# Two transformer blocks on one core: window scores from one key tile, gate tile 0 split on VectorE, bias and meta maps of the differential attention moved on GpSimd

## The reference

```python
def first_block(...):                       # branch a: window and sinks; branch b: top-k over latents
    aq, ak, av, bq, bkv, iq, ik, iw, gates = jnp.split(proj, IN_SPLITS, axis=-1)
    o_a = sliding_window_sink_attention(aq, ak, av, sinks[l], bias_a)
    ik = layer_norm(ik, ...)                # keys of the indexer: logits = iq . ik, relu, weighted sum, top 128
    o_b = indexed_sparse_mla(q_abs, c_kv, iq, ik, iw, w_uv[l], bias_b)
    mixed = gate_a * (o_a @ w_branch_a[l]) + gate_b * (o_b @ w_branch_b[l])

def diff_attn_rows(q1, q2, k1, k2, v, qpos, kpos, key_real, slopes, lam):      # second block, branch a
    bias = -slopes[:, None, None] * (abs(qpos[:, None] - kpos[None, :]) * key_real[None, :])[None]
    s1 = einsum('bqhd,bkhd->bhqk', q1, k1) * scale + bias
    s2 = einsum('bqhd,bkhd->bhqk', q2, k2) * scale + bias
    attn = softmax(s1) - lam * softmax(s2)
    return einsum('bhqk,bkhe->bqhe', attn, v)                     # 4 heads, 4 blocks of 128 rows, 16 + 512 keys

def window_attn_blocks(q, k, v, qpos, kpos, kvalid, kreal, slopes, sink):      # second block, branch b
    # a block of 128 rows sees the 16 meta keys, its own block, the block before and the block after
    s = einsum('bnqgrd,bnkgd->bngrqk', q, k) * scale - slopes * dist           # 8 heads, 2 key groups
    ...
```

## Time and profile before

| | us |
|---|---|
| median of 3 runs | 1560.12 |
| lowest, highest | 1557.65, 1564.45 |
| the profiled execution | 1559.88 |
| its span in the trace | 1558.1 |
| PE busy in the span | 1523.6 (98%) |
| DVE busy | 846.3 (54%) |
| ACT busy | 533.3 (34%) |
| POOL busy | 242.2 (16%) |

### The profile page before, as it was taken

One profiled execution on the slowest core, in us unless ns is written; L12 is line 12 of the kernel. 1 busy time (PEld: TensorE's weight loads), 2 busy tenths in 40 slices (PEclk: granted clock), 3 DMA queues, 4 the chain that ended last, 5 costly groups with the idle time before them and its releaser, 6 DMA issues.

```text
span 1558.1 us, 21063 instructions
## 1 busy us (share of the span) xinstructions
PE 1523.6 (98%) x7388; PEld 1239.9 (80%) x7388; DVE 846.3 (54%) x1519; ACT 533.3 (34%) x942; POOL 242.2 (16%) x190
## 2 busy tenths in 40 slices
PE   7999999999999999999999999999999999999998
PEld 6867887877788888888899778788787888888876
DVE  5577895466555355445854383544655543553454
ACT  5124445523332123222511363444333222221223
POOL 2323334340000000000003473221400000000000
PEclk9999999999999999999999999999999999999999
DMA  6524420023333333332323202111333333333322
GB/s 150 150 54 121 146 62 1 8 88 108 94 94 95 95 94 92 97 92 86 92 86 90 54 15 68 55 54 35 101 95 94 94 96 93 94 94 95 94 81 95
DMA packets 250283, 132.61 MB, mean 85 GB/s; under 512 B 21225, under 2 KB 247653, under 8 KB 250222
## 3 DMA queue, kind: packets, MB, share of 16 engines
q1 hardware_dynamic: 247998, 123.92, 28.0%
q0 software_dynamic: 2144, 7.77, 1.6%
q10 hardware_dynamic: 80, 0.14, 0.0%
HBM read 129.67 MB, written 6.38 MB: 87 GB/s over the span
## 4 chain that ended last, share of the span: by engine, by line
PE 89%; DVE 5%; issue 2%; ACT 1%; DMA 1%; POOL 1%; SPq 0%; DVEq 0%; ACTq 0%; POOLq 0%
PE psL L1715 61%; PE psL L1854 11%; PE psS L1715 5%; PE psT L1863 2%; PE psL L1982 1%; PE psS L2126 1%; PE psS L1959 1%; PE psS L1889 1%; DMA xin<-in_x 1%; PE psS L1902 1%; PE psL L2084 1%; POOL wl L572 1%; PE psS L2103 1%; POOL biasD L650 0%; PE psS L1876 0%
## 5 line engine op out<-in xcount | busy, mean ns | idle before, releaser
L1715 PE MATMUL psL<-hn,wh 128*128 128x512 f32 x1680 | 530.0, 397 | 1.1 <-POOL wl L572 0.9
L1715 PEld LDWEIGHTS psL<-hn,wh 128*128 128x128 f32 x1680 | 314.7, 188 | 77.3 <-issue 1.5
L696 ACT ACTIVATE wh<-stage 128x1024 fp32r<-128x1024 f32 (+3 forms) x250 | 243.3, 973 | 336.8 <-PE psL L1715 244.0
L1715 PE MATMUL psL<-hn,wl 128*128 128x512 f32 x840 | 331.1, 394 | 0.0
L1032 DVE TENSOR_TENSOR wl<-stage,wh 128x1024 fp32r<-128x1024 f32 (+1 forms) x168 | 201.2, 1198 | 92.7 <-ACT wh L696 88.0
L1715 PE MATMUL psL<-hid,wh 128*128 128x512 f32 x704 | 221.6, 395 | 1.3 <-DVE wl L1032 1.3
L572 POOL TENSOR_TENSOR wl<-stage,wh 128x1024 fp32r<-128x1024 f32 (+2 forms) x82 | 156.8, 1912 | 327.0 <-ACT wh L696 327.0
L1715 PEld LDWEIGHTS psL<-hn,wl 128*128 128x128 f32 x840 | 158.5, 189 | 35.6
L1854 PE MATMUL psL<-hn,wh 128*128 128x512 f32 x496 | 172.9, 430 | 1.9 <-POOL wl L572 1.8
L1715 PEld LDWEIGHTS psL<-hid,wh 128*128 128x128 f32 x704 | 131.4, 187 | 35.1 <-DVE wl L1032 3.0
L1715 PE MATMUL psL<-hid,wl 128*128 128x512 f32 x352 | 138.9, 395 | 0.0
(11 more groups left out here) (384 smaller groups left out, 1977.5 us busy)
## 6 DMA issues: line engine op xcount, KB each, us to landing
stage<-in_w_in SPq DMA_DIRECT2D x54, 512.0 KB, 3.9
stage<-in_w_ffn_gate SPq DMA_DIRECT2D x22, 512.0 KB, 3.8
stage<-in_w_ffn_up SPq DMA_DIRECT2D x22, 512.0 KB, 3.8
stage<-in_w_ff_gate SPq DMA_DIRECT2D x22, 512.0 KB, 3.8
stage<-in_w_ff_up SPq DMA_DIRECT2D x22, 512.0 KB, 3.8
stage<-in_w_out SPq DMA_DIRECT2D x16, 512.0 KB, 3.8
stage<-in_w_ffn_down SPq DMA_DIRECT2D x16, 512.0 KB, 3.9
stage<-in_w_ff_down SPq DMA_DIRECT2D x16, 512.0 KB, 3.9
```

The costliest lines, as they stand in the source:

```text
L696: act.activation(wh[:, b, 0:n], stage[:, b, 0:n], ACT.Copy).then_inc(hi[b], 1)
L1715: ins = pe.matmul(dst, w[:, b, k * P:(k + 1) * P], x[:, part, k, c0:c1], start=k + n == 0, stop=k == kc - 1 and n == 2)
```

## The change

**Keys once more.** ACT copies the keys into `kbm`, which is the tile `ikz` of the first block under another name: keys 0 to 255, the 16 meta keys, keys 256 to 511. It does so with three copies between the query projections. The window scores of blocks 0 and 3 are then one matmul of 272 columns from `kbm`.

**Gate tile 0.** In block 1 DVE splits gate tile 0, between the third and fourth eviction of `uq1`, and ACT copies gate tile 1 after the relu of logit 12 instead of at the start of the window loop.

**The differential attention.** `biasD` becomes two tiles, used by even and odd blocks; POOL writes them head by head, six heads ahead of the loop and the rest between other steps, and waits only from block 2 on. The copies into `m8d` move from ACT to POOL, one in each step, and `biasW` is spread between them. On DVE the reciprocal of unit j - 1 goes between the two biased maps of unit j. PE's wait for the last query evictions moves from before the loop to step 3.

```diff
@@ tensors
+        kbm = ikz
+        biasD1, o = at("biasD1", [P, 4, NKEY], o)      # behind vm8, in the space of the gates
-        biasD, o = at("biasD", [P, 4, NKEY], o)
+        biasD0, o = at("biasD0", [P, 4, NKEY], o)
+        biasD = (biasD0, biasD1)
@@ gpsimd, gates of block 1
-                low_pair("gates1", i)
+                if i == 0:
+                    low("gates1", i, 1)
+                else:
+                    low_pair("gates1", i)
@@ gpsimd, block 2
-            def bias_block(i):
-                if i:
-                    pool.wait_ge(ph["df"]["neg"], 8 * i)
-                for h in range(4):
-                    pool.tensor_scalar(biasD[:, h, META:NKEY], dist[...], ..., None, ALU.mult).then_inc(biasD_ok, 1)
+            def bias_unit(j):
+                i, h = divmod(j, 4)
+                if i >= 2:
+                    pool.wait_ge(ph["df"]["neg"], 8 * (i - 1))
+                pool.tensor_scalar(biasD[i % 2][:, h, META:NKEY], dist[...], ..., None, ALU.mult).then_inc(biasD_ok, 1)
+
+            def stack_maps_meta(u):
+                i, h = divmod(u, 4)
+                pool.wait_ge(df_sum, u + 1)
+                if h == 0 and i >= 2:
+                    pool.wait_ge(ph["df"]["pt"], META_TURN[4][i - 2] + 1)
+                pool.tensor_copy(m8d[:, i % 2, h * META:(h + 1) * META], W6[:, u % 3, 0, 0:META]).then_inc(ph["df"]["meta"], 1)
...
-            bias_window(0, NH // 2)
-            bias_block(2)
-            bias_window(NH // 2, NH)
-            bias_block(3)
+            for u in range(2, 16):
+                stack_maps_meta(u)
+                if 4 <= u < 12:
+                    bias_unit(u + 4)
+                elif u < 4:
+                    bias_window(2 * u - 4, 2 * u - 2)
+                else:
+                    bias_window(u - 8, u - 7)
@@ scalar
             high("gates1", 0, 0)
-            relu_of(11, 16)
+            relu_of(11, 13)
+            high("gates1", 0, 1)
+            relu_of(13, 16)
...
+            def middle_meta():
+                act.wait_ge(ev[0], PAIR0["kv2"] + PAIRS["kv2"])
+                act.activation(kbm[:, :, 0:NEAR], kbz[:, :, META:META + NEAR], ACT.Copy)
+                act.activation(kbm[:, :, NEAR:NEAR + META], kbz[:, :, 0:META], ACT.Copy)
+                act.activation(kbm[:, :, NEAR + META:], kbz[:, :, META + NEAR:NKEY], ACT.Copy).then_inc(kbm_ok, 1)
...
-                    act.activation(m8d[:, i % 2, h * META:(h + 1) * META], W6[:, u % 3, 0, 0:META], ACT.Copy).then_inc(p["meta"], 1)
@@ vector
             take_scaled("uq1", 1, 0, qT[:, 2, :], sq[:], QSCALE)
+            low("gates1", 0, 0, ())
             add_logits(11, 12)
...
+                        if m and j:
+                            reciprocal_of(j - 1)
@@ tensor
-            for b in range(2):
-                pe.wait_ge(ev[b], PAIR0["gates2"])
...
+                if j == 3:
+                    for b in range(2):
+                        pe.wait_ge(ev[b], PAIR0["gates2"])
...
+                    if i == 0:
+                        keys = kbm[:, h // 4, 0:NEAR + META]
+                    elif i == NB - 1:
+                        keys = kbm[:, h // 4, NEAR:NKEY]
+                    elif wcol == META:
+                        keys = k[:, 0:META + W]
                     else:
-                        pe.matmul(psS[:, 2 * (j % 2), mcol:mcol + META], q, k[:, 0:META], start=True, stop=True)
-                        ins = pe.matmul(psS[:, 2 * (j % 2), wcol:wcol + W], q, k[:, k0:k0 + W], start=True, stop=True)
+                        keys = k[:, k0:NKEY + META]
+                    ins = pe.matmul(psS[:, 2 * (j % 2), 0:META + W], q, keys, start=True, stop=True)
```

More of the change, by code:

```diff
@@ L665, in _ @@
             pool.wait_ge(dist_ok, 2)
[L666 to L670, removed]
+            for tile in biasD:
+                pool.memset(tile[:, :, 0:META], 0.0)
+            low("qb2", 0, 0)
+            bias_unit(0)
+            low("qb2", 0, 1)
+            bias_unit(1)
+            low("qb2", 1, 0)
+            bias_unit(2)
+            low("qb2", 1, 1)
+            for j in range(3, 6):
+                bias_unit(j)
+            pool.wait_ge(zeros, 2)
+            stack_maps_meta(0)
+            bias_unit(6)
+            stack_maps_meta(1)
+            bias_unit(7)
             pool.wait_ge(nat_t, 3)
@@ L783, in _ @@
             high("gates1", 0, 0)
-            relu_of(11, 16)
+            relu_of(11, 13)
+            high("gates1", 0, 1)
+            relu_of(13, 16)
             def gate_high(l, j):
                 for step in range(2 * KD):
-                    if GATE_START[l][step] == j:
+                    if GATE_START[l][step] == j and (l == 2 or step):
                         if step % 2 == 0:
@@ L1602, in _, with reciprocal_of @@
             p = ph["df"]
+            def reciprocal_of(u):
+                v.wait_ge(ph["df"]["p"], 2 * u + 2)
+                v.reciprocal(st[:, 6, 0:1], rsum[:, 2 * u + 1:2 * u + 2]).then_inc(recip_ok, 1)
             for j in range(16 + 5):
@@ L1613, in _ @@
                         biased(p, u, as_halves(W6[:, j % 3, m, :], NKEY), two_banks(psS[:, 2 * m:2 * m + 2, :], NKEY),
[L1614 removed]
+                               as_halves(biasD[i % 2][:, h, :], NKEY), -TAKEN, u)
+                if j == 16:
+                    reciprocal_of(15)
                 if 1 <= j < 17:
                     u = j - 1
[L1617 to L1618 removed]
+                    v.wait_ge(recip_ok, u + 1)
                     dv.link(v.scalar_tensor_tensor(out=st[:, 6, 1:2], in0=rsum[:, 2 * u:2 * u + 1], scalar=st[:, 6, 0:1], in1=neglam[:],
@@ L2096, in _ @@
                     k0 = META + P * lo_c
-                    if lo_c == 0 and wcol == META:
-                        ins = pe.matmul(psS[:, 2 * (j % 2), 0:META + W], q, k[:, 0:META + W], start=True, stop=True)
-                    elif k0 + W == NKEY and mcol == W:
-                        ins = pe.matmul(psS[:, 2 * (j % 2), 0:W + META], q, k[:, k0:NKEY + META], start=True, stop=True)
-                    else:
-                        pe.matmul(psS[:, 2 * (j % 2), mcol:mcol + META], q, k[:, 0:META], start=True, stop=True)
-                        ins = pe.matmul(psS[:, 2 * (j % 2), wcol:wcol + W], q, k[:, k0:k0 + W], start=True, stop=True)
+                    if i == 0:
+                        if j == 0:
+                            pe.wait_ge(kbm_ok, 1)
+                        keys = kbm[:, h // 4, 0:NEAR + META]
[3 more added lines that the diff above has]
+                        keys = k[:, 0:META + W]
+                    else:
+                        keys = k[:, k0:NKEY + META]
+                    ins = pe.matmul(psS[:, 2 * (j % 2), 0:META + W], q, keys, start=True, stop=True)
                     ins.then_inc(p["s"], 1)
```

19 lines of the change are left out of this document (7 added, 12 removed).

## The result

The changed kernel takes 1553.11 us (median of 7 runs, 1548.66 to 1555.29), the kernel before 1562.85 in the 7 runs beside it: 0.9942, 95% interval 0.9923 to 0.9961. The same program twice more, on two chips: 0.9958 (0.9944 to 0.9972) and 0.9935 (0.9921 to 0.9949). The kernel before stood 2.7 us higher in those 7 runs than the 1560.12 from which the forecast subtracts, so the ratios are the safer comparison. The profiled execution took 1552.76 us with a span of 1551.0, against 1559.88 and 1558.1.

The account below looks back on a forecast made before the run. PE, busy for 98% of the span, was taken to bound the kernel. Gate tiles 2.6, window scores 3.1 and differential attention 2.8 sum to 8.5 us off 1560.12, giving 1551.6 us; 8-in-10 range 1548.5 to 1556.0.

Parts of the forecast that it names:

- Gate tiles 0 and 1: Block 1: PE's waits of 0.88 and 1.75 us for POOL's splits go entirely, at no cost; 2.6 us.
- Window scores: Block 2's window attention: 16 fused units cost 0.31 instead of 0.52 us, all but the first counting; 3.1 us.
- Rival 3: Window scores: the 16-column matmul already lay beside others, so 0.8 us saved instead of 3.1; 1553.9 us, chance 0.08.
- Differential attention: PE's idle pieces in block 2's differential attention shrink; 2.8 us less, between 1.6 and 3.5.
- The moved wait: Before the first differential score: PE's 0.83 us wait for the last query evictions, moved to step 3, goes; gain 0.8.
- the split out of the loop: Differential attention: PE's 1.36 us wait for DVE's difference map, held by POOL's gate tile split, goes; gain 1.4.
- the small waits: Differential attention: PE's other waits for difference maps and ACT's turned maps shrink; 0.6 us taken of a possible 1.2.
- The clock: Differential and window attention of block 2: granted clock 1.00, full speed, in both, with no change of it taken.
- Rival 1: Differential attention: DVE's factor waits about 1 us in two steps with `biasW` pairs; 2.0 given back, 1553.6 us, chance 0.15.
- Rival 2: POOL misses block 2's gate tile 0, or block 1's earlier split delays sums; 2 to 3 us back, 1554.2, chance 0.14.
- Rival 4: Differential attention: POOL becomes the bound, slower than before, some 1568 us, needing a copy of 2.2 us; chance 0.03.

Follow-up runs that it names:

- the third profile: The changed kernel run a third time, unchanged: 0.9935 (0.9921 to 0.9949), clock 1.00 throughout the differential attention, stage 50.68 us.
- the kernel without PE's 0.40: Changed kernel, but PE's wait before block 2's window loop asks for block 2's normalised output first, the last part one step later: 1551.18 us, 0.9930.

## Why the prediction was right, point by point

The forecast was 1551.6, within 1548.5 to 1556.0, with "faster" the likeliest. The median of 1553.11 lies in the range; the ratio of 0.9942 is just beyond the half per cent, with an interval that reaches to both sides of it, and the two repeats (0.9958 and 0.9935) lie on either side. That it is less than before is clear; that it is more than half a per cent less is not.

- **Gate tiles 0 and 1, 2.6 us.** Right, and low: by their own rows 2.0 us at tile 1, where the wait shown was 1.75, and 1.2 at tile 0 (1.48 to 0.32), where it was 0.88, 3.2 in all. The modelled end of the matmul ahead of each covers the rest of either gap. The times of the steps were as worked out: copy at 114.81 (estimated 115), POOL's split over at 118.32 (118.5), the sum for logit 12 held until 118.88 (118.5), at no cost.
- **Window scores, 3.1 us.** Right: 2.98, and 0.31 us a unit. The first unit's gain came back as a longer wait for `yn`, 0.40 us instead of 0.20, as forecast. Rival 3 falls.
- **Differential attention, 2.8 us.** The mechanisms were right, the size was not. Without the fall of the clock it is 0.9 ahead of the first score and 3.1 in the stage, 4.0, above the upper bound of 3.5. The moved wait gave 0.9 (0.8 predicted), the split out of the loop 1.4 to 1.5 (1.4). For the small waits that leaves 1.6 to 1.7 where 0.6 was taken and 1.2 thought possible: that term was mis-sized. Putting the reciprocal back costs 0.35 of it, putting the copies back on ACT 0.46 (51.03 and 51.14 against 50.68). Its waits in brackets fell by 1.1: the three small ones for the difference map, 0.7, are gone, and of those for ACT's turned maps 0.4 (0.59 to 0.20; the 1.5 of the earlier trace rows is the whole program's, and 0.88 of it lies in block 1). The rest never stood in a bracket: from the kernel before with PE's wait moved to the third profile the shown waits of the stage fell by 2.2 us (3.8 to 1.6), PE's idle time by 2.4 (4.03 to 1.65) and its busy time, for nearly the same number of records, by 0.8, together the 3.1. The likely reason, which no run isolates, is that the modelled end of a matmul reaches into the wait behind it and hides part of it, so that a sum over brackets lacks that part.
- **The clock.** "The granted clock is 1.00 in both, full speed, and I take no change of it" is the step that failed. In the profiles of the changed kernel, two of three, it fell to half for 7.6 us and took 2.6 of the 4.0. What the runs show in its place is a clock that comes and goes between executions of the same program. With the fall the profiled execution is 7.1 us faster than before (8.5 predicted), without it 9.4. The forecast lies between the two by no merit of its own: the small waits gave 1.0 more than predicted and the fall took 2.6.
- **The rest.** Predicted at nothing, 0.5 us come back behind the window loop of block 2 (467.12 to 467.64): it comes in at four tiles of the branch projections, 0.25 us at the first, where PE waits 0.20 for POOL's split, which it did not before. POOL waits there for ACT: ACT's step on `mix` starts 0.40 us behind the DVE instruction that releases it (1083.33 to 1083.73), 0.12 in the kernel before (1091.01 to 1091.13), and the copy of the tile stands behind it. The kernel with the meta copies on ACT doesn't have it (467.12), which cancels the 0.46 that it loses in the stage; but the kernel with the differential part alone doesn't have it either (467.13), and it copies on POOL. Why ACT starts later stays open.
- **Rival 1** (POOL blocks DVE for whole instructions, bias heads too) falls: no PE wait of 1 us appears in the steps with two `biasW` heads. The timelines of POOL and DVE in the kernel after show a factor and a difference that begin inside a bias head:

```profile
910.06 1.49 POOL L657 TENSOR_SCALAR biasD<-dist 128x512 f32<-128x512 f32 x1
```

```profile
911.08 0.21 DVE L1660 SCALAR_TENSOR_TENSOR st<-rsum,st,neglam 128x1 f32<-128x1 f32 x1
911.33 0.77 DVE L1662 SCALAR_TENSOR_TENSOR W<-W,st 128x528 f32<-128x528 f32 x1
```

Both take what they take elsewhere (0.22 and 0.77 us); the factor is over 0.26 us before the head (911.55). The longest factor in the stage of after is 0.55 us, at 927.18, beside the start of a head at 927.22, and it too ends 0.66 before that head does. The weight split, however, did hold DVE to its last 0.02 us. The Trainium skill (SBUF — State Buffer, "SBUF: two separate sides") has exclusion for the whole instruction. The 2.00 us factor beside the split, a POOL instruction with two inputs, agrees with it; the 0.21 us factor inside a bias head, which reads one input, does not.
- **Rival 2** (POOL late in the tail) did not come, but the margin was as thin as stated: predicted 0.2, measured 932.25 against 932.46. In the kernel without PE's 0.40 it was down to 0.08.
- **Rival 4:** a copy takes 0.20 us, a tenth of its point.

## What to carry to other kernels

An instruction that holds another engine costs what is waiting behind that engine: move it to where the held engine has slack. When both the medians and a trace must judge an edit of 1 us, compare stage by stage between landmarks, and read the granted clock of each stage first: one fall of the clock, 2.6 us, was about as large as a whole part of this change. And a chain of small steps can lose more to small waits than its list of waits shows: here the brackets fell by 2.2 us and the stage by 3.1.

## What the runs showed of the hardware

PE's clock fell in a stretch in which PE itself was always busy: 0.55 over 7.6 us. What PE had done in the 4.40 us before was the same with the fall and without it, to 0.01 us of busy time (3.42 and 3.43). The Trainium skill (TensorE: Matmul & The Clock Gate, Part 1: The HAM clock gate (the "warmup" mystery)) says that the monitor behind the clock runs free of the kernel's start, so that one kernel shows different numbers of slow matmuls from run to run. It says so of a kernel's start. Here the low clock came and went 880 us into the program, and is alike in that it varies from run to run: two profiles of one program have it and one doesn't, with 2.6 us between them. Whether that monitor is the cause, no run here shows.

What stays open is whether the new order makes the fall likelier. It shows in six of ten profiles of kernels with the new differential attention (in one of them shorter) and in none of four with the old. The old order idles more at that place (0.83, 0.77 and 0.18 us, against 0.80 and 0.18), so a plain lack of work doesn't explain it. The mean granted clock of whole executions speaks against a large difference: it is 0.9960 over 55 executions of kernels with the new order and 0.9961 over 87 with the old. One such fall lowers it by 0.0022 (7.6 x 0.45 of 1551 us; the two profiled executions have 0.995 with it and 0.997 without), so that a fall in six of ten would lower the mean by 0.0013 if nothing else differed. But the difference varies from chip to chip, from 0.0010 lower to 0.0010 higher with the new order, and falls at other places enter it. Fourteen profiles are too few to settle it, and no run was made that could set the moment at which the stage begins.
